# The router's remaining steps spread between the first expert's weight splits, and the next expert's rows loaded 24 halves in, in a two-block model on one core

## What is computed

```python
def moe_swiglu(x, w_router, w_gate, w_up, w_down):
    logits = (x @ w_router).astype(jnp.float32)
    top_val, top_idx = lax.top_k(logits, TOP_K)          # TOP_K = 2
    wts = jax.nn.softmax(top_val, axis=-1)
    gates = jnp.sum(jax.nn.one_hot(top_idx, N_EXPERTS) * wts[..., None], axis=-2)
    out = jnp.zeros_like(x)
    for e in range(N_EXPERTS):                           # 8, each 1024 x 3584
        h = jax.nn.silu(x @ w_gate[e]) * (x @ w_up[e])
        out = out + gates[..., e:e + 1] * (h @ w_down[e])
    return out
```

## Time and profile before

| | us |
|---|---|
| median of 3 runs (lowest, highest) | 1764.91 (1762.72, 1766.04) |
| the profiled execution, its own time | 1764.59 |
| its span | 1762.6 |
| TensorE busy | 1657.1 (94%) |
| VectorE busy | 1373.8 (78%) |
| ScalarE busy | 1031.0 (58%) |

### The profile page before, as it was taken

The page is one execution under the profiler, slowest core; times in us unless marked ns, Lnnn a source line. Parts: engine busy times, 40 slices in busy tenths (PEclk is TensorE's granted clock), DMA queues, the critical chain, the costliest instruction groups (busy, mean ns, idle before and its releaser), DMA issues.

```text
span 1762.6 us, 22524 instructions
## 1 busy us (share of the span) xinstructions
PE 1657.1 (94%) x9022; PEld 1378.5 (78%) x9022; DVE 1373.8 (78%) x1252; ACT 1031.0 (58%) x901; POOL 48.3 (3%) x44
## 2 busy tenths in 40 slices
PE   2999999988989999998899999999999999999976
PEld 2988678868869998896788777887778877788754
DVE  7786666675875555668788989989899898988986
ACT  2344344463324333434577887778887788877862
POOL 0000002000000000000100000000000000000010
PEclk8999999999999999999899999999999999999998
DMA  9688245704745646453799999999999999999992
GB/s 365 224 338 332 96 155 190 288 1 159 205 177 209 251 157 237 180 215 144 267 404 370 408 414 418 406 388 416 415 415 409 399 408 405 417 408 378 411 413 98
DMA packets 119663, 528.30 MB, mean 300 GB/s; under 512 B 10288, under 2 KB 16704, under 8 KB 76288
## 3 DMA queue, kind: packets, MB, share of 16 engines
q1 hardware_dynamic: 112704, 512.44, 74.9%
q10 hardware_dynamic: 5520, 9.62, 1.5%
q0 software_dynamic: 1328, 4.73, 0.7%
HBM read 519.84 MB, written 14.25 MB: 303 GB/s over the span
## 4 chain that ended last, share of the span: by engine, by line
PE 59%; DVE 11%; DMA 5%; ACT 3%; issue 1%; POOL 0%; SPq 0%; DVEq 0%; POOLq 0%; ACTq 0%
PE psum L932 15%; PE psum L934 15%; PE psum L933 15%; DVE units L2029 7%; DMA ring<-in_experts 5%; PE psum L1348 3%; PE psum L1349 2%; ACT units L1838 2%; PE psum L1411 1%; PE psum L1259 1%; PE psum L1463 1%; PE psum L1370 1%; PE psum L1400 1%; DVE R L2429 0%; PE psum L1212 0%
## 5 line engine op out<-in xcount | busy, mean ns | idle before, releaser
L2029 DVE TENSOR_TENSOR units<-ring,units 128x2048 fp32r<-128x2048 f32 (+1 forms) x439 | 990.1, 2280 | 232.2 <-ACT units L1566 134.8
L1838 ACT CAST units<-ring 128x2048 fp32r<-128x2048 f32 x320 | 609.5, 1914 | 184.7 <-PE psum L934 108.3
L1566 ACT CAST units<-ring 128x2048 fp32r<-128x2048 f32 (+1 forms) x119 | 218.5, 1880 | 215.3 <-PE psum L934 185.7
L932 PE MATMUL psum<-units,xr 128*128 128x512 f32 x672 | 268.1, 399 | 7.6 <-DVE units L2029 6.1
L934 PE MATMUL psum<-units,xr 128*128 128x512 f32 x672 | 263.6, 392 | 0.0
L933 PE MATMUL psum<-units,xr 128*128 128x512 f32 x672 | 263.6, 392 | 0.0
L932 PE MATMUL psum<-xr,units 128*128 128x256 f32 x864 | 249.1, 288 | 4.5 <-DVE xr L2029 3.2
L933 PE MATMUL psum<-xr,units 128*128 128x256 f32 x864 | 248.0, 287 | 0.0
L934 PE MATMUL psum<-xr,units 128*128 128x256 f32 x864 | 247.9, 287 | 0.0
L932 PE MATMUL psum<-units,H 128*128 128x512 f32 x472 | 186.5, 395 | 4.4 <-DVE H L2029 4.4
L934 PE MATMUL psum<-units,H 128*128 128x512 f32 x472 | 185.0, 392 | 0.0
(11 more groups left out here) (326 smaller groups left out, 1661.4 us busy)
## 6 DMA issues: line engine op xcount, KB each, us to landing
ring<-in_experts SPq DMA_DIRECT2D x336, 1024.0 KB, 10.8
ring<-in_mod_w SPq DMA_DIRECT2D x12, 2048.0 KB, 10.0
ring<-in_ret_w_in SPq DMA_DIRECT2D x11, 2048.0 KB, 10.0
ring<-in_fox_w_in SPq DMA_DIRECT2D x8, 2048.0 KB, 8.7
ring<-in_sc_w_in SPq DMA_DIRECT2D x6, 2048.0 KB, 8.1
ring<-in_ffn_w_gate SPq DMA_DIRECT2D x5, 2048.0 KB, 7.8
ring<-in_ffn_w_up SPq DMA_DIRECT2D x5, 2048.0 KB, 7.9
ring<-in_ffn_w_down SPq DMA_DIRECT2D x5, 2048.0 KB, 9.1
```

Of the source, the lines that this page charges most:

```text
L932: mm(dst, left[0], right[0], start=first, stop=False)
L1566: nc.scalar.copy(dst[0], src).then_inc(unit_high, 3 - len(parts))
L1838: nc.scalar.copy(dst, src).then_inc(unit_high, 1)
L2029: return v.tensor_tensor(dst, src, high.bitcast(F32), ALU.subtract)
```

## The change

Of the routing work only the splitting of the gathered rows stays ahead of the experts. The rest is called from expert 0's loop by `route_further(h)`, after the low part of half h: order and overflow after half 4, gates after 5, `for_last` after 6, places after 7, the two first sums after 9 and 10. VectorE no longer loads `over` into a register ahead of the experts but, like the other engines, behind them. And `ROWS_BEFORE` goes from 16 to 24, for every expert: SP issues the row load 8 halves later in its order. `GATHER_AFTER` stays 18.

```diff
-ROWS_BEFORE = 16
+ROWS_BEFORE = 24
@@ vector engine
+            def route_further(h):
+
+                if h == 4:
+                    experts_in_order()
+                    overflow()
+                if h == 5:
+                    gates()
+                if h == 6:
+                    for_last(slot_of)
+                    for_last(gate_of)
+                if h == 7:
+                    places()
+                if h in (9, 10):
+                    first_sums(h - 9)
+
@@ def expert(e, q, more, number):
                 for h in range(UNITS, EH):
                     low_unit(e, q, h)
+                    if number == 0 and e == 0:
+                        route_further(h)
                     after(h)
@@
             low(e_x[0][1][:, 4:8, :], psum[:, 1, :].rearrange("p (k t) -> p k t", k=4), e_x[0][0][:, 4:8, :]
                 ).then_inc(gather_emptied, 1)
-            gates()
-            experts_in_order()
-            for_last(slot_of)
-            for_last(gate_of)
-            places()
-            for q in range(NT):
-                first_sums(q)
             dve.wait_ge(up_emptied, 2)
-            overflow()
-            dve.wait_ge(sums_begun, NT)
-            sweeps(dve, expert, start_second, dve.value_load(over[0:1, 0:1], min_val=0, max_val=1))
+            sweeps(dve, expert, start_second)
```

## The result

| | before | after |
|---|---|---|
| median, us (lowest, highest, runs) | 1765.47 (1762.72, 1766.11, 4) | 1793.20 (1791.56, 1794.55, 4) |
| ratio, 95% interval | | 1.0155 (1.0141 to 1.0169) |
| profiled execution, its span | 1764.59, 1762.6 | 1792.67, 1790.8 |

The changed kernel is slower by 27.7 us, and by 28.2 in the spans. The forecast was +14.3 (1778.9, with a range of 1765 to 1790): the sign was right, the size about half of what came.

The account below looks back on a forecast made before the run. It took TensorE's stall on VectorE's routing before half 4 as the prize. Routing -1.5, row waits +9.9, clock +5.0, heavy experts 0, register load +0.9 sum to +14.3 on 1764.6: 1778.9 us, range 1765 to 1790.

Parts of the forecast that it names:

- What bounds the kernel: Start of expert 0: TensorE stalls 5.01 us before half 4 on VectorE's routing; with its clock loss 7.8 us.
- part 1: Routing split between low parts in expert 0: stall cut into waits of about 4.6 us, net -1.5 us (-3.1 to +0.2).
- The landing: Moved row load lands when half 23 did before; waits at the turning 3.6, 4.4, 5.2 us in experts 1, 3, 5.
- What passes through: Light experts' row waits reaching the end, less slack in experts 3 and 5: +9.9 us (5 to 13.2).
- rival A: Slack swallows the row waits and the clock stays up: +2.8 us, so 1767; chance 0.13.
- The clock: TensorE's clock falls after each of three light-expert stalls, 1.65 us each: +5.0 us (0 to 8.4).
- The heavy experts: Row waits of 1.3, 1.3, 0.6 us in experts 2, 4, 6 covered by delay already counted: 0, at most +3.2.
- rival C: Late halves 21 and 32 hold up loads, DMA runs dry, heavy waits add, half clock lasts longer: +26, 1791; chance 0.10.
- The sign that I gave: Sign of a right forecast: each pair of a heavy and a light expert about 5 us longer.
- rival B: Row loads land before needed (under 8.9 us after issue in expert 1), so faster: 1762 to 1764, perhaps 1760; chance 0.07.
- Part 3: Register load at the program's end, between VectorE's last result and the last two instructions: +0.9 us (0 to 1.2).

Follow-up runs that it names:

- the experiment: Routing change alone (row load moved in expert 0 only), with VectorE's register load put back into expert 0's loop behind half 14: 1763.62 us, ratio 0.9992.

## Why the prediction was wrong in size

**What bounds the kernel, and part 1: right.** The waits of expert 0 were forecast at 0.3, 0.6, 0.3 and 3.3, and were 0.36, 0.40, under 0.3 and 3.10. The clock loss of 1.6 behind the last did not come in this profile, but came in four others with the same stall, where it was 1.4. Expert 0 ends 1.9 us earlier (forecast 1.5), after an unforecast wait of 0.96 for its rows: they land at 903.05, not 901.5, and TensorE is 2.9 earlier there. That 1.9 is so near to 1.5 is luck: a loss that did not come and a wait that was not forecast about cancel.

**The landing, which I trusted most: 0.5 us late in expert 1, and TensorE 1.9 early.** "The bytes ahead of the moved load are the same as ahead of half 23 before, so it lands when half 23 landed before." The load now stands behind half 23, and lands 1.3 us after it in the light experts and 1.8 or 1.9 in the heavy ones. Half 23 in turn no longer has the rows ahead of it. The trace after, for half 23 and the row load of expert 1, gives 1002.4 + 13.7 = 1016.1 and 1002.83 + 14.5 = 1017.3, where I had 1016.8 for the load:

```profile
L896 SPq DMA_DIRECT2D ring<-in_experts x1: 332/332/332, 1002.4 to 1002.4; - x1
...
DMA to landing us min/median/max: 13.7/13.7/13.7
...
L875 SPq DMA_DIRECT2D x<-x_rows x1: 368/368/368, 1002.8 to 1002.8; - x1
...
DMA to landing us min/median/max: 14.5/14.5/14.5
```

What I had left out is part 1 itself. I took its gain into the sum but let TensorE come to the turning at the old time. TensorE came there 1.9 us earlier, and the load of half 23 was issued 1.9 earlier too, but it landed only 0.7 earlier, about what the row load that is no longer ahead of it takes: the DMA engines were busy throughout (1.01). So in the program after, the gain of part 1 came back as wait in the first light expert. 3.6 + 0.5 + 1.9 = 6.0, which is the wait. Over the light experts: 16.0 measured, against 13.2 forecast.

**What passes through: right.** Expert 5 gave back 2.3 of the 2.8 that I allowed it, and the others next to nothing. So rival A falls (slack swallows the waits).

**The clock: right in mechanism, somewhat small.** Three falls of 1.65 were forecast, four came, and lost 8.2 in place of 5.0. Two of them lasted 5 us. "Each of these three stalls is longer than 3.14, so by the earlier trace rows the clock falls after it" came true, but length is not what decides: 1.72 was followed by a fall, 2.02 and the 3.10 of half 8 were not.

**The heavy experts: the step that failed.** "A light expert that ends 3 us later moves TensorE but not, or less, the DMA queue, which goes on loading meanwhile. So the 1.3, 1.3 and 0.6 are covered [...]: 0." They waited 2.02, 1.72 and 1.29, and expert 4's wait took the clock with it: 2.0 + 3.3 + 1.2 = 6.5 us. The queue does slip. Windows after, in expert 1 just behind its wait, with the DMA share as the last figure but one:

```profile
1022.90:1027.20 4.30, 4.30 (x14) 2.04 (x14) 3.12 (x2) 4.30 (x4) 0.00 (x0) 0.99 0.26 109
1027.20:1028.50 1.30, 1.30 (x4) 0.38 (x3) 1.30 (x2) 0.32 (x1) 0.00 (x0) 1.00 0.00 0
1028.50:1033.30 4.80, 4.80 (x30) 4.24 (x30) 2.66 (x2) 2.18 (x2) 0.00 (x0) 1.00 0.76 280
```

The program before, in the same place of its expert 1:

```profile
1018.00:1022.00 4.00, 4.00 (x11) 1.34 (x11) 4.00 (x4) 3.92 (x5) 0.00 (x0) 1.00 1.02 424
1022.00:1029.00 7.00, 7.00 (x49) 6.37 (x48) 6.83 (x4) 5.64 (x4) 0.00 (x0) 1.00 1.01 421
```

The DMA engines stand still for 0.74 x 4.3 + 1.3 + 0.24 x 4.8 = 5.6 us in one light expert. A place in the ring comes free only when TensorE gets on, directly for an unsplit half and through the four split buffers for the others, and TensorE stood for 6. In the next expert half 23 lands at 1119.0 + 12.2 = 1131.2 instead of 1125.8, 5.4 later:

```profile
L896 SPq DMA_DIRECT2D ring<-in_experts x1: 333/333/333, 1119.0 to 1119.0; - x1
...
DMA to landing us min/median/max: 12.2/12.2/12.2
```

TensorE comes there 6.6 later (1133.14 - 2.02 = 1131.1 against 1124.5), so only 1.2 of the 1.3 is covered, and the 1.8 by which the rows land behind half 23 come on top: 1.3 - 1.2 + 1.8 = 1.9, against 2.02 measured. I had the heavy waits as a bound (+3.2) and in rival C, and put them at nothing for a reason that no row bore out. The delay of the producer and of the consumer is one delay here, because the consumer frees the producer's buffers. The sign that I gave, each pair of a heavy and a light expert about 5 longer, came out at 10.5, 8.6 and 7.2.

**Rival C** gave 1791 with a chance of 0.10, and is nearest. Of its parts the heavy waits and the longer half clock are shown. Its first one, the hold-up of half 28, can be seen in the trace after: that load is issued at 1028.5 and lands 6.1 after half 27, where before it was 2.5. That this adds to the time by itself is not shown: with half 21 out of the way the loads stood still elsewhere, and the heavy waits stayed. As to **rival B**, its turning point (a landing within 8.9 us) is met in ScalarE's queue, with 7.2 to 8.4, and there the loss is indeed gone; in SP's queue it was 14.5, and the load landed between its neighbours there, as I had it. But "A small load takes that long only because it stands behind several megabytes" does not hold: from ScalarE's queue the same loads still took 7.2 to 8.4.

**Part 3, the register load: right, a little small.** +0.9 forecast, 1.4 by the end of the program after, 1.6 by the experiment.

**The sum as measured**, by the marks of the experts: -1.9 (expert 0) + 19.8 (light experts; waits 16.0 and clock 6.5, less the 2.3 of expert 5, and 0.4 of scatter) + 6.5 (heavy; waits 5.0, clock 1.65) + 2.4 (expert 7) + 1.4 (the register load) = 28.2. Of the 13.9 that the forecast of 14.3 lacks, 6.5 are the heavy experts, 4.9 the light ones, 2.4 expert 7 and 0.5 the register load, less 0.4 in expert 0.

**Left open.** The 2.4 of expert 7, which has no row load. From the end of expert 6 to the end of the span it is 133.0 us after and 129.2 before. Less 1.5 where the register load is at the end, the program before and the twelve experiments lie between 127.6 and 130.5, and after at 131.5. The trace shows where it arises. SP issues halves 8 to 16 of expert 7 all 24.4 us later than before, but they land over 27.4 us (1661.3 to 1688.7) instead of 24.5 (1637.2 to 1661.7), with the DMA engines busy throughout, and from there on the loads are 26.8 late. ScalarE stands for halves 13 and 14:

```profile
1680.79 1.91 ACT L1838 CAST units<-ring 128x2048 fp32r<-128x2048 f32 x1 [1.88 <-DMA ring<-in_experts]
1683.73 1.91 ACT L1838 CAST units<-ring 128x2048 fp32r<-128x2048 f32 x1 [1.04 <-DMA ring<-in_experts]
```

TensorE's waits of 0.85 and 0.83 follow from these. The same halves take 23.6 to 24.8 us to land in eleven of the experiments, and 26.1 in the row load alone, so it may be the scatter of one execution. Why these transfers were slower no run shows.

## What to carry to other kernels

A load that is put further back in a full queue lands later by the loads that now stand ahead of it (here eight of 1 MB, in expert 1 1017.3 instead of 996.9), and the wait is paid in full where the waiting engine is busy throughout. Compare its new landing with the moment of use before moving it, with the gain of the other parts of the change taken off that moment, or move the use as well (here four halves later, at no cost). Do not count a delay of the consumer as cover for later loads when the consumer itself frees the buffers that the loads go into: the queue then slips with it. And a wait on TensorE can cost more by the clock behind it: here nothing behind 2.02 us, 1.65 behind 1.72, 2.7 behind 6.0.

## What the runs showed of the hardware

- **The same stall costs or does not.** The wait of 3.1 us before half 8 was followed by 3.4 us at 1.2 GHz in four profiles (the routing change alone, the row load in ScalarE's queue, the unsplit half moved, the load at 16) and by full clock in six, the program after among them. In the program after, a wait of 1.72 was followed by 1.2 GHz, and one of 2.02 by full clock. With the unsplit half moved it was the other way: a wait of 2.02 was followed by 3.4 us at 1.2 GHz, and one of 2.37 by full clock. The program around the wait was nearly the same each time, so its length alone does not decide; what does is not shown. The Trainium skill (TensorE: Matmul & The Clock Gate, section on the HAM clock gate) speaks of a free-running monitor, and the traces agree in so far as a like wait costs or not. For the wait before half 8 that makes 1.4 us of scatter: 4.25 us from the start of half 8 to the first turn in the four, 2.81 to 2.85 in the six.
- **A queue of its own is worth 3.5 to 6.2 us to a small load.** The row load takes 11.5 to 14.5 us from SP's queue (the program after) and 7.2 to 8.4 from ScalarE's, with the same weight loads beside it.
- **A register load at the end of VectorE's work** takes 0.55 us by itself, but the next instruction starts 1.6 later than without it.
